# Three more weight slabs of the dense layers multiplied in blocks, and the work around them put elsewhere

## What is computed

```python
def squared_relu_mlp(x, w1, w2):                 # w1 1024x4096, w2 4096x1024
    return jnp.square(jax.nn.relu(x @ w1)) @ w2

def mamba2_bidir_mixer(x, w_in, conv_w, conv_b, dt_bias, a_log, d_skip, norm_w, w_out):
    zxbcdt = x @ w_in
    z, xbc, dt = jnp.split(zxbcdt, [SSM_D_INNER, SSM_D_INNER + SSM_CONV_DIM], axis=-1)
    xbc = jax.nn.silu(depthwise_conv_centred(xbc, conv_w, conv_b))   # 5 taps along the tokens
    ...
# first_block, layer i of 2
x = layer_norm(DN_ALPHA * x + mix, ln1_g[i], ln1_b[i])
x = layer_norm(DN_ALPHA * x + squared_relu_mlp(x, mlp_w1[i], mlp_w2[i]), ln2_g[i], ln2_b[i])
# second_block, layer l of 2
mod = silu(c) @ ada_w[l] + ada_b[l]
sh1, sc1, gt1, sh2, sc2, gt2 = jnp.split(mod, 6, axis=-1)
```

## Time and profile before

| | us |
|---|---|
| median of the runs (2290.45 to 2292.6) | 2290.61 |
| profiled execution, whole time | 2294.64 |
| profiled execution, span | 2292.7 |
| TensorE busy | 2260.5 |
| VectorE busy | 1044.3 |
| ScalarE busy | 464.0 |

### The profile page before, as it was taken

The page is one execution under the profiler, slowest core; times in us unless marked ns, Lnnn a source line. Parts: engine busy times, 40 slices in busy tenths (PEclk is TensorE's granted clock), DMA queues, the critical chain, the costliest instruction groups (busy, mean ns, idle before and its releaser), DMA issues.

```text
span 2292.7 us, 26577 instructions
## 1 busy us (share of the span) xinstructions
PE 2260.5 (99%) x11222; PEld 1372.7 (60%) x11222; DVE 1044.3 (46%) x2045; ACT 464.0 (20%) x1038; POOL 74.1 (3%) x130
## 2 busy tenths in 40 slices
PE   9999999999999999999999999999999999999998
PEld 6568547886497459997444333335999643333333
DVE  3578646668588557675211111124767411111122
ACT  2411003258111011230211111101122121111111
POOL 2000000000000000000000000000000000000000
PEclk9999999999999999999999999999999999999999
DMA  7279725354689415236999999994423899999997
GB/s 294 110 300 383 290 78 205 148 184 170 244 352 391 179 71 193 97 147 280 415 428 428 427 428 427 428 419 184 172 86 122 365 420 428 427 427 428 427 428 288
DMA packets 59173, 671.72 MB, mean 293 GB/s; under 512 B 7505, under 2 KB 7793, under 8 KB 18721
## 3 DMA queue, kind: packets, MB, share of 16 engines
q1 hardware_dynamic: 51888, 649.45, 68.9%
q0 software_dynamic: 7152, 20.43, 2.7%
HBM read 666.59 MB, written 3.26 MB: 292 GB/s over the span
## 4 chain that ended last, share of the span: by engine, by line
PE 88%; DMA 9%; DVE 2%; issue 0%; ACT 0%; SPq 0%; POOL 0%; DVEq 0%; POOLq 0%; ACTq 0%
PE ps L101 85%; DMA ring<-in_exp_w 5%; DMA arena<-in_exp_w 4%; PE ps L349 1%; DVE arena L117 1%; DMA arena<-ssm_rows 1%; PE ps L2978 1%; DVE arena L114 0%; PE ps L638 0%; DMA ring<-in_attn_w_in 0%; PE ps L2128 0%; DVE X L117 0%; PE ps L1326 0%; ACT arena L106 0%; PE ps L2953 0%
## 5 line engine op out<-in xcount | busy, mean ns | idle before, releaser
L101 PE MATMUL ps<-arena 128*128 128x128 f32 (+6 forms) x4452 | 1004.6, 448 | 14.2 <-DMA arena<-in_exp_w 5.5
L101 PEld LDWEIGHTS ps<-arena 128*128 128x128 f32 (+2 forms) x4452 | 509.1, 170 | 464.8 <-issue 434.4
L101 PE MATMUL ps<-ring,arena 128*64 128x512 f32 (+2 forms) x1720 | 461.0, 584 | 2.0 <-DMA ring<-in_exp_w 1.2
L101 PE MATMUL ps<-XTGB,ring 128*128 128x256 f32 (+1 forms) x2064 | 393.2, 346 | 0.0
L101 PEld LDWEIGHTS ps<-XTGB,ring 128*128 128x128 f32 x2064 | 341.9, 191 | 47.0 <-issue 10.7
L101 PEld LDWEIGHTS ps<-ring,arena 128*64 128x64 f32 (+1 forms) x1720 | 174.0, 150 | 259.3 <-issue 255.0
L122 DVE COPY arena<-ps 128x512 f32<-128x512 f32 (+5 forms) x133 | 63.3, 496 | 406.7 <-PE ps L101 287.9
L121 ACT COPY arena<-ps 128x512 f32<-128x512 f32 (+2 forms) x186 | 84.6, 473 | 686.9 <-PE ps L2978 284.3
L101 PE MATMUL ps<-XTGB,arena 128*128 128x128 f32 (+2 forms) x752 | 190.4, 407 | 0.0
L117 DVE TENSOR_TENSOR arena<-ps,arena 128x256 f32<-128x256 f32 (+5 forms) x283 | 124.6, 478 | 123.4 <-PE ps L101 93.1
L101 PE MATMUL ps<-ring,XTGB 128*128 128x512 f32 (+3 forms) x484 | 170.4, 507 | 2.7 <-DMA ring<-in_attn_w_in 2.5
(11 more groups left out here) (154 smaller groups left out, 1000.3 us busy)
## 6 DMA issues: line engine op xcount, KB each, us to landing
arena<-in_exp_w SPq DMA_DIRECT2D x90, 2048.0 KB, 27.3
ring<-in_exp_w SPq DMA_DIRECT2D x68, 2048.0 KB, 28.0
ring<-in_mlp_w SPq DMA_DIRECT2D x25, 2048.0 KB, 11.9
ring<-in_ada_w SPq DMA_DIRECT2D x20, 2048.0 KB, 9.4
XTGB<-in_exp_w SPq DMA_DIRECT2D x18, 2048.0 KB, 32.3
ring<-in_ssm_w_in SPq DMA_DIRECT2D x12, 2048.0 KB, 7.5
ring<-in_w_in SPq DMA_DIRECT2D x12, 2048.0 KB, 8.0
ring<-in_gate_w SPq DMA_DIRECT2D x12, 2048.0 KB, 8.1
```

Source lines behind the costliest of these rows:

```text
L101: return self.e.matmul(o, lhsT=lhsT, rhs=rhs, start=start, stop=stop, skip_group_check=True)
```

## The change

1. Slab 6 of the first matrix of layer 0 is done in blocks. The last modulation sum on TensorE stands behind slab 7, in both layers, not inside it. The addition of the bias (`ada_out`) stands behind the first block sums on VectorE. The second set of block sums gets another place, where the activation sums lay, so that it need not wait for the stored modulation.
2. In the convolution stage slabs 5 and 6 are done in blocks by new functions of the same form (`sw_x_sums`, `sw_sums`, `sw_last_sum`, `sw_products`, `sw_results`). ScalarE copies their first product (`first_product`); there are four `s_u` buffers, and the results are built up in them.
3. The row scalings move from the end of layer 0 behind convolutions 10 and 12. The four parameter loads move from the convolution stage to `mlp0_pool`, and `next_gb` behind the store of the decay rows.

```diff
-            if n == 7:
-                v.wait_ge(at("ada mm", l, 2), at("ada_b", l))
...
+        def ada_out(v, l, ab):
+            v.wait_ge(at("ada mm", l, 2), at("ada_b", l))
...
-        W1_BLOCKS = (2, 4), (2, 4, 6)
+        W1_BLOCKS = (2, 4, 6), (2, 4, 6)
...
-                        gemm_f(pe, ("m1", l, s), ("m1", l, s), 4, mid=(lambda: ada_pe(pe, l, 8, acc)) if s == 7 else None)
+                        gemm_f(pe, ("m1", l, s), ("m1", l, s), 4)
...
+            ada_pe(pe, l, 8, acc)
...
             v.wait_ge(at("h", l, s))
-            if s == 1:
-                v.wait_ge(at("mod", l))
...
             block_sums(v, l, 0, hT, sA, sB)
+            ada_out(v, l, ab)
             for s in range(1, NS):
...
             ada_b_pool(pool, 0, ab0)
+            pool.landed(pool.e.dma_start(prm, d["ssm_conv"].rearrange("p (a b) -> p a b", a=32)), "ssmp", "ssmp")
+            pool.landed(pool.e.dma_start(dd, d["ssm_dn"]), "ssmp", "ssmp")
+            pool.landed(pool.e.dma_start(dtb, bcast(d["ssm_dt_bias"][0:1, :])), "ssmp", "ssmp")
+            pool.landed(pool.e.dma_start(ang, bcast(d["ssm_A_log"][0:1, :])), "ssmp", "ssmp")
             keep_mod(pool, 0)
...
-            next_gb(pool, "ln1_g", "ln1_b", 1, 1, "ln3", at("x gb", 2, 1))
...
                 norm_turned(v, 2, t)
-            norm_rows_all(v, 2, at("gb", "ln2"))
+            sw_x_sums(v)
+            sw_sums(v, 5)
+            sw_last_sum(v, 5)
+            sw_sums(v, 6)
...
-        s_u = [arena.get(2, 260) for _ in range(2)]
+        s_u = [arena.get(2, 260) for _ in range(4)]
...
+        def sw_sums(v, s):
+            w = weights(("sw", s))
+            s1, s2 = swS[s % 2]
+            v.wait_ge(at("w", ("sw", s)))
+            k = v.then_inc(v.tt(s1, w[:, 0:4, T:2 * T], w[:, 4:8, T:2 * T], ALU.add), ("swS", s, 5))
+            v.wait_ge(k)
+            k = v.then_inc(v.tt(s2, s1, w[:, 0:4, 0:T], ALU.subtract), ("swS", s, 6))
+            v.then_inc(v.tt(w[:, 0:4, T:2 * T], w[:, 0:4, 0:T], w[:, 0:4, T:2 * T], ALU.subtract), ("swS", s, 7))
+        def sw_last_sum(v, s):
+            s1, s2 = swS[s % 2]
+            v.wait_ge(at("swS", s, 6), at("swp", s - 1, 2) if s == 6 else None)
+            v.then_inc(v.tt(swS4, weights(("sw", s))[:, 4:8, 0:T], s2, ALU.subtract), ("swS", s, 3))
+        def sw_products(pe, s):
...
+            pe.wait_ge(at("w", ("sw", s)), at("swX"))
+            for r, group in enumerate(SW_GROUPS):
+                ps = bank(pe, "swp", s, r)
+                for n, p in enumerate(group):
+                    x, y = pairs[p]
+                    if p in (3, 5, 6, 7):
+                        pe.wait_ge(at("swS", s, p))
+                    for f in range(2):
+                        for c in range(4):
+                            ins = pe.mm(ps[:, n * T + f * P:n * T + (f + 1) * P], y[:, c, f * P:(f + 1) * P], x[:, c, :],
+                                        c == 0, c == 3)
+        def sw_results(v, s, r):
...
+            v.wait_ge(at("swp", s, r))
+            if r == 0:
+                v.wait_ge(at("swP1", s))
+                plus(c12, 0, 1, c11, ("swU2", s))
...
+            if s < 7:
+                sw_products(pe, s)
+            else:
+                gemm_f(pe, ("sw", s), ("sw", s), 4)
...
+            first_product(5)
...
+                if n == 3:
+                    first_product(6)
...
+            for r in range(4):
+                sw_results(v, 5, r)
             for n, i in enumerate(CONV):
                 conv(n, i)
+                if n == 0:
+                    sw_last_sum(v, 6)
+                if n == 2:
+                    for r in range(3):
+                        sw_results(v, 6, r)
+                if n == 3:
+                    sw_results(v, 6, 3)
+                if n in (10, 12):
+                    norm_rows(v, 2, n // 2 - 5, at("gb", "ln2"), at("xt", 2, n // 2 - 5, 0), at("xt", 2, n // 2 - 5, 4))
```

More of the change, by code:

```diff
@@ L836, in ada_dve @@
                     between()
-            if n == 7:
-                v.wait_ge(at("ada mm", l, 2), at("ada_b", l))
[L839 to L842, removed]
+        def ada_out(v, l, ab):
+            v.wait_ge(at("ada mm", l, 2), at("ada_b", l))
+            for j in range(4):
+                o = slice(32 * j, 32 * j + 3)
+                v.then_inc(v.tt(modc[l][o, :], ps_of("ada", l)[o, :], ab[o, :], ALU.add), ("modc", l),
+                           ("read", "ada", l))
         def ada_pe(pe, l, n, acc):
@@ L1257, in build, with conv_in, sw_x_sums @@
         drow = nc.dram_tensor("ssm_rows", (16, 1024), F32).ap()
+        room = arena.pos
+        arena.pos = zT.shape[1] * T + xcT.shape[1] * T
+        swX = [arena.get(4, P) for _ in range(4)]
+        swS = [[arena.get(4, T) for _ in range(2)] for _ in range(2)]
+        swS4 = arena.get(4, T)
+        arena.pos = room
+        SW_GROUPS = ((1, 6), (5, 7), (3, 4), (2,))
+        def conv_in(n):
+            return s_u[n % 2 + (2 if n in (4, 5) else 0)]
+        def sw_x_sums(v):
+            x1, x2, x3, x4 = swX
+            v.wait_ge(at("XT", 2, 0), at("XT", 2, 1))
+            k = v.then_inc(v.tt(x1, XT[:, 0:4, P:T], XT[:, 0:4, 0:P], ALU.subtract), "swX")
+            v.then_inc(v.tt(x3, XT[:, 4:8, P:T], XT[:, 0:4, P:T], ALU.subtract), "swX")
+            v.wait_ge(k)
+            k = v.then_inc(v.tt(x2, XT[:, 4:8, P:T], x1, ALU.subtract), "swX")
+            v.wait_ge(k)
+            v.then_inc(v.tt(x4, XT[:, 4:8, 0:P], x2, ALU.subtract), "swX")
@@ new lines, in sw_product, with sw_parts, plus @@
+        def sw_product(s, r, n):
+            return ps_of("swp", s, r)[:, n * T:(n + 1) * T].rearrange("p (f t) -> p f t", f=2)
+        def sw_parts(s):
+            n = 0 if s == 5 else 4
+            return [conv_in(n + k)[:, :, o:o + P] for k in range(2) for o in (2, 2 + P)]
+        def sw_results(v, s, r):
+            c11, c12, c21, c22 = sw_parts(s)
+            def plus(o, q, n, x, *done):
+                return v.then_inc(v.tt(o, sw_product(s, q, n), x, ALU.add), ("read", "swp", s, q), *done)
+            v.wait_ge(at("swp", s, r))
+            if r == 0:
+                v.wait_ge(at("swP1", s))
+                plus(c12, 0, 1, c11, ("swU2", s))
+            elif r == 1:
+                v.wait_ge(at("swU2", s))
+                e = plus(c21, 1, 1, c12)
+                plus(c12, 1, 0, c12, ("swU4", s))
+                v.wait_ge(e)
+                plus(c22, 1, 0, c21, ("conv in", s, 1), ("swU3", s))
+            elif r == 2:
+                v.wait_ge(at("swU3", s), at("swU4", s))
+                plus(c12, 2, 0, c12, ("conv in", s, 0))
+                plus(c21, 2, 1, c21, ("conv in", s, 1))
+            else:
+                plus(c11, 3, 0, c11, ("conv in", s, 0))
@@ L1434, in ssm_act @@
                 s, fp, f0 = 4 + i // 2, i % 2, 2 * i
[L1435 to L1436 removed]
+                u, v_ = conv_in(n), s_v[n % 2]
+                if n == 3:
+                    first_product(6)
                 if n >= 2:
                     act.wait_ge(at("conv", CONV[n - 2]))
[L1439 to L1440 removed]
+                if s in (5, 6):
+                    act.wait_ge(at("conv in", s, fp), at("xc", CONV[n - 2]) if n >= 2 else None)
+                else:
+                    act.wait_ge(at("sw", s, fp))
+                    k = act.then_inc(act.cp(u[:, :, 2:258], two(ps_of("sw", s, fp))), ("read", "sw", s, fp))
+                    act.wait_ge(k)
                 for q in range(2):
```

29 lines of the change are left out of this document (18 added, 11 removed).

## The result

The changed kernel is slower: 2298.22 us (median of 20 runs, 2294.06 to 2303.05) beside 2292.54 for the kernel before beside it (20 runs, 2290.45 to 2297.14). The ratio is 1.0025, 95% interval 1.0019 to 1.0031. I had forecast 3.8 us less; it is 5.7 us more.

The account below looks back on a forecast made before the run. TensorE, busy 99% of the span, was taken to bound the kernel. Gains of 1.1 (dense stage), 0.1 (layer 1) and 2.6 (convolution stage) sum to 3.8 us: median 2286.9 us, range 2285.4 to 2289.9.

Parts of the forecast that it names:

- the last sentence of the sum: Stages behind the change: they move along with TensorE's and VectorE's progress, so the 3.8 us gain reaches the end.
- everything behind unchanged in length: Sign in the changed kernel's trace: stages after the convolution stage keep their lengths and only start earlier.
- rival (d): Scan behind the change: its few short waits shrink by 1 us, or runs come out well; gain 4.8, 2285.8; chance 0.15.
- A slab in blocks: TensorE, dense and convolution stages: 112 half-wide entries take 12.60 us behind another shape, where a whole slab takes 13.91.
- Dense stage: Layer 0, slab 6 to the second weight matrix: TensorE gains 1.1 us, with ends 0 and 1.4.
- wait at the modulation sum: Dense stage, about 242 us: TensorE waits 0.3 us for VectorE's piece 11; over 1.5 would refute the forecast.
- piece 10's load: Dense stage: modulation weights issued at about 220.75 take 7.4 us and land at 228.2.
- Convolution stage: Slabs 5 and 6 in blocks: TensorE gains 1.27 + 1.3 = 2.6 us, with ends 0 and 2.6.
- no wait from 345 to 400 us: Sign in the convolution stage: TensorE never stands still there, despite VectorE's added sums.
- The sum I called the narrowest place: Convolution stage: VectorE's last sum for slab 6 ends at 379.7, needed at 381.2; 1.5 us left, priced at nothing.
- Rival (b): Convolution stage: VectorE's added 11.4 us falls behind the last slab, last convolution ending after 470.7; 2298; chance 0.05.
- Rival (c): Blocked slabs: half-wide matmuls wait out their weight loads, 21.4 us a slab; 2313, or 2302 by the skill page; chance 0.01.

Follow-up runs that it names:

- e2: Kernel before with eight never-run matmuls added in the skipped path of layer 0; 2299.44 us, ratio 1.0028.
- e4: Changed kernel with two never-run matmuls added in the skipped path of layer 0; 2290.07 us, ratio 0.9991.
- e12: e4 with the skipped, never-run path of layer 1 made 64 matmuls shorter; 2288.37 us, ratio 0.9986 to the kernel before.
- e14: Kernel before with only the dense half of the change, plus 64 never-run matmuls in layer 1's skipped path; 2292.88 us, ratio 1.0007.
- e3: Changed kernel with one never-run matmul added in the skipped path of layer 0; 2295.39 us, ratio 1.0021.
- e7: Kernel before with 60 never-run matmuls added in the skipped path of layer 0; 2293.51 us, ratio 1.0008.
- e8: Kernel before, unchanged, profiled in one more execution; weight loads 7.6 us, scan waits 1.26 us.
- e9: Changed kernel, unchanged, profiled in one more execution; weight loads 8.5 us, scan waits 2.57 us, two stalls (4.07 and 4.73 us).
- e13: Kernel before with only the convolution half of the change, layer 1's skipped path 64 matmuls shorter; 2290.34 us, ratio 0.9997.

## Why the prediction was wrong

- **The step that failed** is the last sentence of the sum: "Later stages, loads included, are started by TensorE's and VectorE's own progress, so I let them move along." They were not only started by it. Two things far from the change depend on how long the program is: where a packet of code is cut behind the jump at 1550 us (6.2 us there in the trace; e2 and e4 carry it both ways), and how long many of SyncE's weight loads take (1.5 us in the scan; e12 and e14 carry loads and waits both ways). Together they are 7.7 of the 9.5 us between the forecast (3.8 less) and the result (5.7 more); the 1.7 us of clock in layer 1 is seen in the profiled execution, and how many of the other runs have it is not known. So the sign "everything behind unchanged in length" failed. None of my rivals was about code; my rival (d) let the scan's waits shrink, and they grew.
- **The local terms held.** A slab in blocks: 12.60 forecast, 12.56 measured. Dense stage: 1.1 forecast, 0.9 measured, with a wait at the modulation sum of 0.44 for 0.3, because piece 10's load took 8.1 us where I had taken 7.4 (it landed at 226.8, or 228.4 without the 1.6 us of the start; I had 228.2). In e12, with the shorter program, it took 7.4 and TensorE waited 0.21. Convolution stage: 2.6 forecast and measured, no wait from 345 to 400 us. The sum I called the narrowest place ended at 378.5, 1.3 us ahead of TensorE's fifth product (379.87); I had 1.5.
- **Rival (b) did not come.** Its price, 2298, is the measured median (2298.22) by luck: its sign, the last convolution ending later than 470.7, is not there. VectorE's last convolutions start at 461.60 and end at 465.7, 5.0 us earlier than before, 3.4 without the start of the program. This timeline row of the changed kernel answers to the last of the earlier trace rows:

```profile
461.60 4.13 DVE L114 SCALAR_TENSOR_TENSOR arena<-arena 128x256 f32<-128x256 f32 x8 [2.85 <-ACT arena L105]
```

- **Rival (c), half-wide matmuls bound by their weight loads, did not come**, as slab 4 had said: 112 ns an entry in all three new slabs.
- **The forecast itself** was 3.8 us off the median, a ratio of 0.9984 (2286.9 to 2290.61). (By its own terms, 2290.61 less 3.8, it is 2286.8; I wrote 0.1 too much.) With the second stall and the slower loads taken away (e12) the same work gives 0.9986 (0.9977 to 0.9995). So the sum agrees, within some 2 us, for the work, and was wrong for the program.

What stays open: why a longer TensorE program makes SyncE's loads slower, why some loads (`in_gate_w`) are not touched, and at which length it sets in; I know only that 96 instructions more left them at 7.5 us and 192 more did not. Whether it is the length itself, or something that changes with it, as where the program and its weights come to lie in memory, no run here tells apart. Whether code of other engines does the same wasn't tried.

## What to carry to other kernels

A kernel of thousands of unrolled instructions with a jump in it has a term that no stage shows: look in the profile for "issue" waits of TensorE behind jumps, count the instructions that run between the first and a possible second, and treat that remainder as part of the change's price, since any edit ahead of it moves it. When a change adds or removes code, compare the same loads' time from issue to landing far from the change. Before a loss of 1 to 2 us in one profiled execution is laid to a stage, look at the granted clock there. And before a slower result is laid to the work, add a few never-run instructions to both kernels: here that told some 7 us of code placement from some 4 us of work.

## What the hardware showed that I had not expected

- Behind this jump TensorE stood still for 4.0 to 4.8 us until the code was there, of which about 1 us was not covered by the layer norm in the changed kernel, and for a second 4.7 to 5.4 us where the rest of the first packet held six, five or two instructions (after, e2, e3). With 53 or more left (e7) there was no second stall, nor with the 37 of the kernel before. Where between 6 and 37 it sets in was not tried.
- The second stall also kept TensorE's clock at the 1.2 GHz level for longer: 6.8 us with one (3.4 in e8), 13.7 with two (10.2 in e3 and e9).
- Most 2 MB weight loads that meet an empty queue between 90 and 900 us take about 7.5 us in some programs and 8.1 to 8.6 in others, the same in a second execution of four programs, and 256 TensorE instructions that are never run move a program from one to the other (e12 and e14; in e13 one load of three in the scan stayed at 8.8).
